# Turning and splitting the second layer's keys and queries in the latent stage instead of in the head loop

## The chip, the cores and the metric

The kernel runs on one core of a Trainium2 chip. The metric is the device time of one execution in microseconds; lower is better. The engines that matter are TensorE (PE; its weight loads are shown apart as PEld), VectorE (DVE), ScalarE (ACT), GpSimd (POOL) and SyncE (SP), which here does nothing but issue DMAs. ScalarE issues some DMAs as well, in line with its own work.

## What is computed

One step of a transformer trunk of two layers on 592 tokens: 512 prompt tokens, 64 sample tokens and 16 meta tokens. Layer 0 is a forgetting attention (16 heads of width 64) and an MLP. Layer 1 is a latent attention and an MLP. All of it is in f32, and every large product is made from operands split into a high and a low fp32r part, in three passes (high by high, high by low, low by high). Cut to what the change touches:

```python
def mla_shared_latent(x, kv_norm, w_kv_down, ckv_norm, pos):
    z = rmsnorm(x, kv_norm) @ w_kv_down
    ckv = rmsnorm(z[..., :KV_RANK], ckv_norm)            # KV_RANK = 256
    krope = rope(z[..., KV_RANK:], pos)                  # 32 columns, shared by all heads
    return ckv, krope
def mla_decompress(ckv, w_kv_up):
    kv = (ckv @ w_kv_up).reshape(bsz, t, MLA_HEADS, MLA_NOPE + MLA_V)   # 16, 64 + 64
    return kv[..., :MLA_NOPE], kv[..., MLA_NOPE:]
def mla_queries(h, w_q_down, q_norm, w_q_up, pos):
    cq = rmsnorm(h @ w_q_down, q_norm)                   # 384 columns
    q = (cq @ w_q_up).reshape(bsz, t, MLA_HEADS, MLA_NOPE + MLA_ROPE)   # 16, 64 + 32
    return q[..., :MLA_NOPE], rope(q[..., MLA_NOPE:], pos)
...
logits = (q_nope @ k_nope.T + q_rope @ k_rope.T) * MLA_SCALE
p = softmax(where(mask, logits, NEG));  o = p @ v;  x = x + o @ w_o_b
```

With the 256 cached rows there are 848 keys. The 592 query rows are worked in five units a head: four of 128 prompt rows and one of 80 (the sample and meta rows).

## The kernel before

Every engine runs a program of its own, in an order written out by hand, and the programs meet through semaphores. Large weights come in pieces j through four raw slots (`slot_of`); ScalarE makes the high part (`hi`), VectorE the low part (`lo`). Both layers run `attention(layer)` on each engine; only the step of a head differs.

**Layer 0.** The keys and queries of a head already lie turned (width on the partitions, tokens along the row) and split in DRAM (`k_turned`, `q_turned`). SP's `fox_head` loads kh, qh, kl and ql for head h into one of three slots, once TensorE is done with the head that had the slot. The step is `fox_step`: per head five score units, six groups of transposes of the probabilities, and the weighted sums of the heads before, all interleaved. Values of a pair of heads come straight from the cache and the outputs (`fox_v`, four DMAs, issued by ScalarE in the middle of a pair), and GpSimd splits them (`split_v`).

**Layer 1, latent stage.** After layer 0's MLP the stage makes the compressed latent and turns it (`ckvTh`, `ckvTl`). Then TensorE runs 28 products: for two weight pieces, seven token tiles by two blocks of 512 columns, tokens on the partitions, keys and values of a head side by side. ScalarE copies each out of PSUM to one of four slots of `stn`, and SP stores it to `kv_mla` in DRAM. After that fifteen transposes turn the query latent (`cqTh`, `cqTl`), and 20 products (four weight pieces by five token tiles, 384 columns, four heads each) give the queries; VectorE applies the rotary turn in `stn` with six small instructions, and SP stores to `q_mla`. At the end the rotary key `krn` is turned and copied into rows 64 to 95 of both kh slots.

**Layer 1, head loop.** SP loads natural rows for each pair of heads (`mla_q`, two DMAs; `mla_kv`, three, keys and values together). In `mla_step`, TensorE turns the next head's queries and keys with `prep`, twelve transposes in three groups, ScalarE copies each group (high part) and VectorE subtracts (low part). With the six groups of the probabilities these are the nine groups a head (`GROUPS = (6, 9)`). The steps run in hardware loops over the pairs. The output weights (`load_wo`) are loaded ahead of the loop.

## Time and profile before

| | |
|---|---|
| median of three runs | 1565.55 us (1563.05 to 1568.0) |
| profiled execution | 1566.23 us, span 1564.1 us, mean granted TensorE clock 0.972 |
| TensorE busy | 1480.1 us (95%), weight loads 1413.8 us (90%) |
| VectorE busy | 1081.4 us (69%) |
| ScalarE busy | 729.8 us (47%) |
| GpSimd busy | 432.4 us (28%) |
| DMA | 164.18 MB, mean 105 GB/s |

Times are positions on the profiled execution's clock or lengths in it, in us. The layers lie one after the other: attention of layer 0 about 185 to 360, its MLP after it, the latent stage of layer 1 from about 850, its attention about 947 to 1110, and the last MLP up to the end. The busy shares are means over all of these; the change touches the latent stage and the attention of layer 1 alone, so the views of those stretches are what counts. A row names the engine, the line of the kernel, the operation and its tiles (out <- in); PEclk is the granted clock as a share of full speed.

### The profile page before, as it was taken

Reading aid. Unit: us, or ns where it says so; the run is one execution under the profiler, and the core shown is the slowest. Engines: PE = TensorE matmul, PEld = TensorE weight load, DVE = VectorE, ACT = ScalarE, POOL = GpSimd, SP = SyncE. Lnnn points to the kernel's source line nnn. Section 1 sums busy time; section 2 is a strip of 40 time slices with the busy share of each in tenths; the row PEclk is TensorE's granted clock in tenths of the full one; section 3 lists DMA queues with packets and bytes.
Section 4 is the critical chain, followed back from the end, with each engine's and each line's share of the span. In section 5 each row is a group of like instructions: output and inputs, shape, how many; then the busy total and the mean of one; then the engine's idle time right before and its main releaser. Section 6 shows DMA issues by size and latency. Waiting matters only on the chain.

```text
span 1564.1 us, 29635 instructions
## 1 busy us (share of the span) xinstructions
PE 1480.1 (95%) x10389; PEld 1413.8 (90%) x10389; DVE 1081.4 (69%) x1962; ACT 729.8 (47%) x1510; POOL 432.4 (28%) x437
## 2 busy tenths in 40 slices
PE   8999988889899999999999997999989999999997
PEld 6788977779899999999988786999989999999997
DVE  5224267656987778787784156998598877878775
ACT  6234158754453433434252435998444343343434
POOL 0000047743422212222020004667342222222200
PEclk9999989989999999999999998999999999999998
DMA  8257566651131322313130637320022132231211
GB/s 289 99 145 210 147 186 167 165 138 48 55 109 55 106 92 68 107 54 107 56 132 19 227 121 201 94 77 1 29 81 99 64 107 82 78 107 64 97 54 61
DMA packets 129720, 164.18 MB, mean 105 GB/s; under 512 B 11936, under 2 KB 98912, under 8 KB 129648
## 3 DMA queue, kind: packets, MB, share of 16 engines
q1 hardware_dynamic: 124176, 160.62, 33.1%
q10 hardware_dynamic: 5472, 2.61, 0.9%
q8 instruction: 44, 0.72, 0.2%
q14 instruction: 28, 0.23, 0.0%
HBM read 132.52 MB, written 30.68 MB: 104 GB/s over the span
## 4 chain that ended last, share of the span: by engine, by line
PE 66%; issue 9%; DVE 7%; ACT 3%; DMA 3%; SPq 1%; POOL 1%; ACTq 0%; POOLq 0%; DVEq 0%
PE ps L2403 25%; PE ps L2434 21%; PE ps L1971 11%; PE ps L2137 3%; PE ps L2206 2%; PE ps L2250 1%; PE ps L2252 1%; SPq L574 1%; DMA ql<-q_turned 1%; DMA natv<-in_cache_v 1%; DVE wul L1701 1%; DVE wul L1410 1%; DVE bl L1747 1%; ACT pth L1085 1%; PE ps L2177 1%
## 5 line engine op out<-in xcount | busy, mean ns | idle before, releaser
L1799 DVE TENSOR_TENSOR xT<-xT,ps 128x592 f32<-128x592 f32 (+1 forms) x256 | 194.8, 761 | 49.0 <-PE ps L2403 47.2
L803 POOL TENSOR_TENSOR prob<-prob,rs 128x144 f32<-128x144 f32 (+4 forms) x160 | 119.4, 757 | 248.1 <-DVE rs L1562 246.5
L2434 PE MATMUL ps<-bh,wuh 128*128 128x296 f32 (+1 forms) x512 | 153.3, 299 | 8.6 <-DVE wul L1701 5.0
L2434 PE MATMUL ps<-bl,wuh 128*128 128x296 f32 (+1 forms) x512 | 152.9, 299 | 0.0
L2434 PE MATMUL ps<-bh,wul 128*128 128x296 f32 (+1 forms) x512 | 152.6, 298 | 0.0
L893 POOL TENSOR_TENSOR ssum<-raw 128x512 f32<-128x512 f32 x32 | 48.9, 1528 | 292.6 <-DMA raw<-in_w_up 290.1
L1572 DVE TENSOR_TENSOR ptl<-ps,pth 128x256 fp32r<-128x256 f32 (+2 forms) x192 | 96.1, 502 | 45.3 <-ACT pth L1085 44.6
L2403 PE MATMUL ps<-hh,dn2h 128*128 128x296 f32 (+1 forms) x512 | 111.6, 299 | 0.6 <-DVE xT L1799 0.3
L1267 ACT ACTIVATE snap<-ps 128x296 f32<-128x296 f32 (+1 forms) x32 | 13.2, 412 | 210.4 <-PE ps L2434 210.4
L2403 PE MATMUL ps<-hl,dn2h 128*128 128x296 f32 (+1 forms) x512 | 110.3, 296 | 0.0
L2403 PE MATMUL ps<-hh,dn2l 128*128 128x296 f32 (+1 forms) x512 | 110.2, 296 | 0.0
L2434 PEld LDWEIGHTS ps<-bh,wuh 128*128 128x128 f32 x512 | 96.7, 189 | 10.3 <-ACT snap L1267 4.5
L1085 ACT ACTIVATE pth<-ps 128x256 fp32r<-128x256 f32 (+2 forms) x192 | 84.4, 450 | 39.2 <-PE ps L2206 30.6
L1701 DVE TENSOR_TENSOR wul<-raw,wuh 128x512 fp32r<-128x512 f32 x128 | 97.4, 780 | 0.1
L2434 PEld LDWEIGHTS ps<-bh,wul 128*128 128x128 f32 x512 | 97.1, 190 | 0.0
L2434 PEld LDWEIGHTS ps<-bl,wuh 128*128 128x128 f32 x512 | 97.0, 189 | 0.0
L1255 ACT ACTIVATE hh<-hu 128x592 fp32r<-128x592 f32 (+1 forms) x64 | 44.4, 693 | 107.4 <-DVE hu L1786 107.4
L1971 PE MATMUL ps<-wh,xgh 128*128 128x512 f32 (+5 forms) x240 | 92.0, 383 | 2.5 <-DVE xT L1799 2.2
L1075 ACT ACTIVATE prob<-ps,nmx 128x144 f32<-128x144 f32 (+4 forms) x160 | 85.5, 535 | 18.5 <-DVE nmx L1556 15.2
L1971 PE MATMUL ps<-wl,xgh 128*128 128x512 f32 (+5 forms) x240 | 90.3, 376 | 0.0
L1971 PE MATMUL ps<-wh,xgl 128*128 128x512 f32 (+5 forms) x240 | 89.8, 374 | 0.0
L1556 DVE TENSOR_REDUCE nmx<-ps 128x1 f32<-128x144 f32 (+4 forms) x160 | 77.3, 497 | 15.4 <-PE ps L1971 14.4
(284 smaller groups left out, 4589.8 us busy)
## 6 DMA issues: line engine op xcount, KB each, us to landing
raw<-in_w_up SPq DMA_DIRECT2D x32, 1024.0 KB, 7.2
raw<-in_w_down SPq DMA_DIRECT2D x32, 1024.0 KB, 5.0
raw<-in_w_in_a SPq DMA_DIRECT2D x12, 1024.0 KB, 8.5
kh<-k_turned SPq DMA_DIRECT2D x32, 212.0 KB
k_turned<-kst SPq DMA_DIRECT2D x48, 128.0 KB, 2.5
kv_mla<-stn SPq DMA_DIRECT2D x24, 256.0 KB, 2.1
q_turned<-qst SPq DMA_DIRECT2D x32, 148.0 KB, 3.1
qh<-q_turned SPq DMA_DIRECT2D x16, 296.0 KB
```

Of the source, the lines that this page charges most:

```text
L803: g.tensor_tensor(prob[c][0:rows, off:off + n], prob[c][0:rows, off:off + n], rs[0:rows, u:u + 1].to_broadcast([rows, n]), ALU.mult).then_ ...
L893: g.tensor_tensor(ssum[:, 1 + 2 * par, :, :], a11, a21, ALU.subtract).then_inc(s_ready, 1)
L1075: s.activation(form(prob[c][0:rows, off:off + n]), src, ACT.Exp, bias=nmx[0:rows, u:u + 1], accum_out=sm[0:rows, u:u + 1]).then_inc(exp_do ...
L1085: s.activation(dst, src, ACT.Copy).then_inc(g_hi, 1)
L1556: v.tensor_reduce(nmx[0:rows, u:u + 1], logits(u)[0], AX.XY if u == NT - 1 else AX.X, ALU.max, negate=True).then_inc(max_done, 1)
L1572: v.tensor_tensor(dst, src, hi_part.bitcast(F32), ALU.subtract).then_inc(g_lo, 1)
L1701: v.tensor_tensor(up_unit(wul, u), up_source(u, par), up_unit(wuh, u).bitcast(F32), ALU.subtract).then_inc(ul_done, 1)
L1799: v.tensor_tensor(a, a, two_banks(2 + m % 2, n), ALU.add).then_inc(x_ready if last else acc_done, 1)
L1971: return te.matmul(out, a, b, start=start, stop=stop)
L2137: i = te.matmul(ps[:, 2 * q_banks(j) + t, 0:TH], w, x[:, k, TH * t:TH * t + TH], start=(k == 0 and p == 0), stop=(k == KD - 1 and p == 2), ...
L2403: i = te.matmul(ps[:, 2 * pair + t, 0:n // 2], w[:, k, c], x[:, k, t * (n // 2):(t + 1) * (n // 2)], start=(k == 0 and p == 0), stop=(k == ...
L2434: i = te.matmul(ps[:, bank, 0:h], w[:, k, :], x, start=(u not in (3, 4, 6) and k == 0 and p == 0), stop=(k == 3 and p == 2), skip_group_ch ...
```

## The change

The columns of `w_kv_up` and `w_q_up` are put in another order as the inputs are laid out, so that two heads' keys, two heads' plain queries, or four heads' rotary halves are 128 neighbouring columns. The key and query products then take the weights as the stationary operand and the latent as the moving one, so their results come out already turned: [128 = two heads of 64, 848 keys] and [128, 592 queries]. The values keep the old form.

**The stage** becomes one list, `LATENT`, of 34 items: eight key blocks (k) and fourteen value blocks (v) in turns, then four times two plain query blocks (n) and a rotary block (r). They use three pairs of PSUM banks, and an item waits for the item three before. For k and n ScalarE copies the high part and VectorE subtracts, into `lkst` (two slots) and `lqst` (three slots). For r VectorE does three multiplications by a table from DRAM (`rope`), an addition and, after ScalarE's copy, the subtraction. SP stores each k, n and r with four DMAs to `kTm`, `qTm` and `qRm`, each v with one to `v_mla`. The query latent is turned between the items 11, 13 and 15; the rotary key after 22, and its copies into three kh and kl slots come at item 23. SP's list has more in it: at item 27 it waits for the stores so far and loads heads 0 to 2, at item 30 the first two value pairs.

**The loop** drops `prep` and its groups, and both layers use one step in the order of `fox_step`, unrolled, with three slots of kh, kl, qh and ql. A head takes eight loads (`mla_head`), issued by SP when the head that had its slot has its scores. Value pairs from the third on are issued by ScalarE in the middle of a pair (`mla_v`, three DMAs). `load_wo(1)` comes after the last head's loads, its last three pieces after the last scores.

```diff
-GROUPS = (6, 9)
+GROUPS = (6, 6)
...
+        LATENT = []
+        for half in range(2):
+            LATENT += [(kind, i + (4 if kind == "k" else 7) * half) for kind, i in
+                       (("k", 0), ("v", 0), ("k", 1), ("v", 1), ("v", 2), ("k", 2), ("v", 3), ("v", 4), ("k", 3), ("v", 5), ("v", 6))]
+        for g in range(4):
+            LATENT += [("n", 2 * g), ("n", 2 * g + 1), ("r", g)]
+        LAST = {10: 0, 21: 1, 24: 2, 27: 3, 30: 4, 33: 5}
...
+        def lat_pair(n):
+
+            return (0, 1, 3)[n % 3]
...
             def load_wo(layer):
-                if layer == 1:
-                    sp.wait_ge(lo_done, W_END)
                 for m in range(KD):
-                    if layer == 0 and m == 5:
-                        sp.wait_ge(s_ps, 5 * (HEADS - 1))
+                    if m == 5:
+                        sp.wait_ge(s_ps, 5 * HEADS * layer + 5 * (HEADS - 1))
...
+            def mla_head(h, c):
+
+                sp.dma_start(kh[c][0:HD, :].bitcast(F32), kTm[0][h]).then_inc(kq_in[c], 16)
+                sp.dma_start(qh[c][0:HD, :].bitcast(F32), qTm[0][h]).then_inc(kq_in[c], 16)
+                for x in range(2):
+                    r = HD + 16 * x
+                    sp.dma_start(qh[c][r:r + 16, :].bitcast(F32), qRm[0][x, 16 * h:16 * h + 16, :]).then_inc(kq_in[c], 16)
+                sp.dma_start(kl[c][0:HD, :].bitcast(F32), kTm[1][h]).then_inc(kq_in[c], 16)
+                sp.dma_start(ql[c][0:HD, :].bitcast(F32), qTm[1][h]).then_inc(kq_in[c], 16)
+                for x in range(2):
+                    r = HD + 16 * x
+                    sp.dma_start(ql[c][r:r + 16, :].bitcast(F32), qRm[1][x, 16 * h:16 * h + 16, :]).then_inc(kq_in[c], 16)
...
+            for n, (kind, i) in enumerate(LATENT):
...
+                if kind == "v":
+                    t, c = i % 7, 512 * (i // 7)
+                    rows = TX if t == NT else P
+                    r0 = P * t if t <= NT else T + P * (t - 5)
+                    sp.wait_ge(v_evac, i + 1)
+                    sp.dma_start(v_mla[r0:r0 + rows, c:c + 512], stn[0:rows, i % 3, :]).then_inc(lv_out[i % 3], 16)
+                    continue
+                sp.wait_ge(kq_lo, kind_count("knr", n))
+                q = kind_count("nr", n) - 1
+                for low in range(2):
+                    if kind == "k":
+                        for p in range(2):
+                            sp.dma_start(kTm[low][2 * i + p], lkst[HD * p:HD * p + HD, i % 2, low, :].bitcast(F32)).then_inc(
+                                lk_out[i % 2], 16)
+                    elif kind == "n":
+                        for p in range(2):
+                            sp.dma_start(qTm[low][2 * i + p],
+                                         lqst[HD * p:HD * p + HD, q % 3, low, :].bitcast(F32)).then_inc(lq_out[q % 3], 16)
+                    else:
+                        for p in range(2):
+                            sp.dma_start(qRm[low][p, HD * i:HD * i + HD, :],
+                                         lqst[HD * p:HD * p + HD, q % 3, low, :].bitcast(F32)).then_inc(lq_out[q % 3], 16)
+                if n == 27:
+                    for i_ in range(2):
+                        sp.wait_ge(lk_out[i_], 64 * 4)
+                    for i_ in range(3):
+                        sp.wait_ge(lq_out[i_], LQ_COUNT[5][i_])
+                    sp.wait_ge(half_used, QU0 + 2)
+                    sp.wait_ge(kr_lo, 1)
+                    for h in range(3):
+                        mla_head(h, key_slot(h))
+                if n == 30:
+                    for i_ in range(3):
+                        sp.wait_ge(lv_out[i_], 16 * len(range(i_, 14, 3)))
+                    mla_v(sp, 0, 0, natv1[0])
+                    mla_v(sp, 1, 1, natv1[1])
...
-            mla_q(0, 0)
-            sp.wait_ge(kr_ps, 1)
-            mla_kv(1, 1)
-            mla_q(1, 1)
+            for i in range(3):
+                sp.wait_ge(lq_out[i], LQ_COUNT[11][i])
+            for h in range(3, HEADS):
+                sp.wait_ge(s_ps, 5 * HEADS + 5 * (h - 2))
+                mla_head(h, key_slot(h))
             load_wo(1)
...
+                for j in range(1, PAIRS - 1):
+                    step(2 * j, 0, j)
+                    act.wait_ge(v_split, PAIRS * layer + j)
+                    if layer == 0:
                         fox_v(act, j + 1, (j + 1) % 2, natv0[(j + 1) % 2])
-                        step(2 * j + 1, 1, j)
-                else:
-                    with act.Fori(1, PAIRS - 1) as i:
-                        step(2 * i, 0, i)
-                        step(2 * i + 1, 1, i)
+                    else:
+                        mla_v(act, j + 1, (j + 1) % 2, natv1[(j + 1) % 2])
...
+                    wait_lat(act, n)
...
+                    s.activation(lkst[:, i % 2, 0, 336:KEYS], ps[:, b, :], ACT.Copy)
+                    s.activation(lkst[:, i % 2, 0, 0:336], ps[:, b + 1, 0:336], ACT.Copy).then_inc(kq_hi, 1)
+                elif kind == "v":
...
+                if n == 23:
+                    act.wait_ge(kr_ps, 1)
+                    act.wait_ge(half_used, QU0)
+                    act.wait_ge(lo_done, QU0 + 2)
+                    for sl in range(3):
+                        s.activation(kh[sl][HD:R_MLA, 336:KEYS], pf[0:ROPE, 2048:2560], ACT.Copy)
+                        i_ = s.activation(kh[sl][HD:R_MLA, 0:336], pf[0:ROPE, 2560:2896], ACT.Copy)
+                    i_.then_inc(kr_T, 1)
...
+                elif kind == "r":
+                    wait_lat(dve, n)
+                    dve.wait_ge(rope_tab, 16)
+                    if i:
+                        dve.wait_ge(kq_lo, kind_count("knr", n) - 3)
+                    two = two_banks(lat_pair(n), T)
+                    for rows, src, tab, dst in ((slice(0, P), slice(0, P), 0, ra), (slice(0, HD), slice(HD, P), 1, rb),
+                                                (slice(HD, P), slice(0, HD), 1, rb)):
+                        v.scalar_tensor_tensor(halves(dst[rows, :]), two[src], MLA_SCALE, halves(rope[rows, tab, :]),
+                                               ALU.mult, ALU.mult).then_inc(qr_mul, 1)
+                    dve.wait_ge(qr_mul, 3 * i + 3)
+                    v.tensor_tensor(ra[:], ra[:], rb[:], ALU.add).then_inc(qr_ready, 1)
+                    dve.wait_ge(kq_hi, kind_count("knr", n))
+                    v.tensor_tensor(lqst[:, q % 3, 1, :], ra[:], lqst[:, q % 3, 0, :].bitcast(F32), ALU.subtract).then_inc(kq_lo, 1)
...
+            def latent_free(m):
+
+                kind, i = LATENT[m]
+                if kind == "v":
+                    pe.wait_ge(v_evac, i + 1)
+                elif kind == "r":
+                    pe.wait_ge(qr_mul, 3 * i + 3)
+                else:
+                    pe.wait_ge(kq_lo, kind_count("knr", m))
+
+            pe.wait_ge(zT_lo, 2)
...
-
-            pe.wait_ge(kr_ready, 1)
-            for t in range(NT):
-                te.transpose(pf[0:ROPE, 3072 + P * t:3072 + P * t + P], krn[:, t, :], ident)
-            for t in range(2):
-                te.transpose(pf[0:ROPE, 3584 + P * t:3584 + P * t + P], krn[:, 5 + t, :], ident)
-            te.transpose(pf[0:ROPE, 3840:3920], krn[0:TX, NT, :], ident[0:TX, 0:TX]).then_inc(kr_ps, 1)
+                if n == 22:
...
+                        return lambda k: view(w, j)[:, k, 512:1024]
+                    o = tokens_product(ps[0:r, bank, :], ((lambda k: ckvTh[:, k, c0:c0 + r]), (lambda k: ckvTl[:, k, c0:c0 + r])),
+                                       (values(wh), values(wl)), 2, r, 512)
+                else:
+                    def weights(w, k):
+                        a = view(w, j)[:, k, :]
+                        b = i % 4 if kind == "k" else 2 if kind == "r" else i % 2
+                        return a[:, P * b:P * b + P]
+                    x_h, x_l = (ckvTh, ckvTl) if kind == "k" else (cqTh, cqTl)
+                    spans = (slice(0, SEQ), slice(SEQ, KEYS)) if kind == "k" else (slice(0, TH), slice(TH, T))
+                    k_n = 2 if kind == "k" else 3
+                    for k in range(k_n):
+                        for p, (w, x) in enumerate(((wh, x_h), (wh, x_l), (wl, x_h))):
+                            for b, c in enumerate(spans):
+                                o = te.matmul(ps[:, bank + b, 0:c.stop - c.start], weights(w, k), x[:, k, c],
+                                              start=(k == 0 and p == 0), stop=(k == k_n - 1 and p == 2), skip_group_check=True)
+                o.then_inc(half_used if n in LAST else lat_ps, 1)
+                if n in (11, 13, 15):
+                    latent_query((n - 11) // 2)
+                if n == 22:
+                    turn_rope_keys()
...
+    kv = [h * 2 * HD + v * HD + d for g in range(2) for v in range(2) for h in range(8 * g, 8 * g + 8) for d in range(HD)]
+    q = []
+    for g in range(4):
+        heads = range(4 * g, 4 * g + 4)
+        q += [h * R_MLA + d for h in heads for d in range(HD)]
+        q += [h * R_MLA + HD + x * (ROPE // 2) + d for x in range(2) for h in heads for d in range(ROPE // 2)]
```

Each `...` above leaves lines out. `latent_query`, `turn_rope_keys` and `latent_free` are TensorE's; the first two hold the fifteen and the seven transposes of the code before.

## Rows read from the trace of the kernel before

**Rows 1.** Chain of waits that ended last: start us, length us, engine, tile, line.

```profile
196.14 6.58 PE ps L2137 x48
...
859.79 40.56 PE ps L1971 x168
```

**Rows 2.** Timeline of ScalarE: start us, length us, instruction, [idle before <- releaser].

```profile
333.76 1.06 ACT L970 ACTIVATE wuh<-raw 128x1024 fp32r<-128x1024 f32 x1 [1.55 <-DMA raw<-in_w_o_a]
...
952.76 0.38 ACT L1075 ACTIVATE prob<-ps,nmx 128x144 f32<-128x144 f32 x1 [2.28 <-DVE nmx L1556]
```

**Rows 3.** Timeline of TensorE; L1971 with a [idle] note is a head's first score.

```profile
325.72 0.34 PE L1971 MATMUL ps<-kh,qh 128*128 128x144 f32 x1 [1.33 <-DMA ql<-q_turned]
...
960.30 0.30 PE L1971 MATMUL ps<-kh,qh 96*128 96x144 f32 x1 [1.09 <-ACT prob L1075]
...
970.01 0.60 PE L2221 MATMUL ps<-cst,natq 128*96 128x128 f32 x4
...
970.76 0.36 PE L2250 MATMUL ps<-pth,vlh 128*128 128x256 f32 x1
...
1080.36 0.31 PE L1971 MATMUL ps<-kh,qh 96*128 96x144 f32 x1
```

**Rows 4.** Busy time by stretch: layer 0's heads 3 to 14, layer 1's 2 to 14, two steps of layer 0.

```profile
core 0: us, PE busy (x) PEld busy (x) DVE busy (x) ACT busy (x) POOL busy (x), PEclk, DMA share, GB/s
225.58:325.72 100.14, 86.73 (x675) 76.17 (x673) 74.24 (x208) 76.85 (x218) 70.56 (x98) 0.98 0.67 165
967.94:1080.36 112.42, 112.08 (x965) 107.98 (x964) 103.14 (x274) 103.86 (x287) 76.56 (x106) 1.00 0.21 64
233.80:240.98 7.18, 6.70 (x59) 6.25 (x58) 6.03 (x18) 6.35 (x19) 4.86 (x6) 1.00 0.60 155
240.98:250.16 9.18, 7.42 (x59) 6.17 (x57) 6.13 (x18) 6.36 (x18) 7.36 (x12) 1.00 0.70 173
```

**Rows 5.** Waits between 200 and 336 us: total us, times, longest us.

```profile
POOL vlh L826 <- DMA natv<-in_cache_v: 12.3, 6, 3.6
```

**Rows 6.** DMA issues of the page: KB each, median us from issue to landing.

```profile
natk<-kv_mla SPq DMA_DIRECT2D x8, 512.0 KB, 4.0
...
natv<-in_cache_v ACTq DMA_DIRECT2D x6, 128.0 KB, 13.6
...
q_turned<-qst SPq DMA_DIRECT2D x32, 148.0 KB, 3.1
qh<-q_turned SPq DMA_DIRECT2D x16, 296.0 KB
```

**Rows 7.** Groups by line and form: busy us, mean ns of one | idle before.

```profile
L1668 DVE TENSOR_TENSOR kl<-ps,kh 32x512 fp32r<-32x512 f32 x2 | 1.4, 677 | 0.2 <-ACT kh L1353 0.2
...
L1670 DVE TENSOR_TENSOR kl<-ps,kh 32x336 fp32r<-32x336 f32 x2 | 1.0, 488 | 0.0
...
L1352 ACT ACTIVATE kh<-ps 32x512 fp32r<-32x512 f32 x2 | 1.2, 578 | 0.2 <-PE ps L2553 0.2
...
L1391 DVE TENSOR_TENSOR wl<-raw,wh 128x1152 fp32r<-128x1152 f32 x4 | 5.2, 1350 | 0.0
...
L1786 DVE SCALAR_TENSOR_TENSOR hu<-hu,rT 128x592 f32<-128x592 f32 x32 | 26.7, 835 | 1.1
```

**Rows 8.** Timeline of SyncE's queue: start us, length of the issues us, tiles, count.

```profile
185.34 2.39 SPq L633 DMA_DIRECT2D q_turned<-qst  x4
187.90 0.48 SPq L521 DMA_DIRECT2D natv_first<-out_o_v_p  x1
...
196.57 0.42 SPq L524 DMA_DIRECT2D natv_first<-in_cache_v  x1
...
249.40 0.45 SPq L621 DMA_DIRECT2D kh<-k_turned  x1
249.89 0.60 SPq L622 DMA_DIRECT2D kh<-k_turned  x1
...
976.86 0.37 SPq L668 DMA_DIRECT2D natq<-q_mla  x1
```

**Rows 9.** Chain of waits: last partial sum of either attention.

```profile
354.05 1.44 POOL ol L845
...
1103.12 1.44 POOL ol L845
```

More of the change, by code:

```diff
@@ L719, in _ @@
             sp.dma_start(gq[:], io["q_norm"].partition_broadcast(P)).then_inc(rope_in, 16)
-            for j in range(QU0, W_END):
+            for j in range(QU0, QU0 + 2):
                 load(j)
@@ L1100, in out, with step @@
                     s.activation(corr[rows, :], pf[0:HD, 3072:3072 + T], ACT.Copy).then_inc(o_corr, 1)
-                def fox_step(h, c, pair, first=False, last=False):
+                def step(h, c, pair, first=False, last=False):
                     if first:
-                        act.wait_ge(half_used, KVD0 - 1)
+                        act.wait_ge(half_used, W_END if layer else KVD0 - 1)
                         for u in range(3):
                             exp(h, c, u)
-                        query_hi(PAIRS - 1)
+                        if layer == 0:
+                            query_hi(PAIRS - 1)
                         exp(h, c, 3)
@@ L1126, in fox_step @@
                     exp(h, c, 4)
-                def mla_step(h, c, pair, first=False, last=False):
-                    if not first:
-                        turned(h, 0)
-                    exp(h, c, 0)
-                    if not first:
-                        turned(h, 1)
-                    if not last:
-                        qk(h, 0, 1 - c)
-                        qk(h, 1, 1 - c)
-                    else:
-                        wo_high(layer, 0)
-                    exp(h, c, 1)
-                    if not first:
-                        turned(h, 2)
-                    if not (isinstance(h, int) and h < 2):
-                        out(h - 2, c, pair - 1)
-                    if not last:
-                        qk(h, 2, 1 - c)
-                    exp(h, c, 2)
-                    if not first:
-                        turned(h, 3)
-                    exp(h, c, 3)
-                    if not first:
-                        turned(h, 4)
-                        turned(h, 5)
-                    exp(h, c, 4)
-                step = mla_step if layer else fox_step
-                for k in range(3 * layer):
-                    qk(-1, k, 0)
                 step(0, 0, 0, first=True)
@@ L1355, in _ @@
+            for i in range(3):
+                act.wait_ge(lq_out[i], LQ_COUNT[11][i])
             attention(1)
@@ L1586, in out, with step @@
                                     ALU.subtract).then_inc(o_lo, 1)
-                def fox_step(h, c, pair, first=False, last=False):
+                def step(h, c, pair, first=False, last=False):
                     if first:
@@ L1592, in fox_step @@
                         clear_prob()
[L1593 removed]
+                        if layer == 0:
+                            query_lo(PAIRS - 1)
                         recip(h, 0)
@@ L1662, in clear_prob @@
                         v.memset(prob[c][:, P_OFF[NT] + 336:P_OFF[NT] + 384], 0.0).then_inc(p_zero, 1)
-                if layer == 1:
-                    clear_prob()
-                    dve.wait_ge(kr_T, 1)
-                    for sl in range(2):
-                        v.tensor_tensor(kl[sl][HD:R_MLA, 336:KEYS], pf[0:ROPE, 3072:3584],
-                                        kh[sl][HD:R_MLA, 336:KEYS].bitcast(F32), ALU.subtract)
-                        i = v.tensor_tensor(kl[sl][HD:R_MLA, 0:336], pf[0:ROPE, 3584:3920],
-                                            kh[sl][HD:R_MLA, 0:336].bitcast(F32), ALU.subtract)
-                    i.then_inc(kr_lo, 1)
-                step = mla_step if layer else fox_step
-                for k in range(3 * layer):
-                    qk(-1, k, 0)
                 step(0, 0, 0, first=True)
@@ L2263, in rest, with step @@
                 def rest(h, part, pair, vs, p):
-                    groups = p_split(layer, h - 1, 4 if part < 3 else 5) + G0
+                    groups = p_split(h - 1, 4 if part < 3 else 5) + G0
                     weighted_v(h - 2, part, groups, pair, vs, p)
-                def fox_step(h, c, pair, nat, turn=0, first=False, last=False):
+                def step(h, c, pair, nat, first=False, last=False):
                     if first:
-                        pe.wait_ge(kq_in[key_slot(0)], 80)
+                        pe.wait_ge(kq_in[key_slot(0)], kq_count(0))
                         for u in range(3):
                             scores(h, c, u)
-                        query_block(PAIRS - 1)
+                        if layer == 0:
+                            query_block(PAIRS - 1)
                         scores(h, c, 3)
```

522 lines of the change are left out of this document (201 added, 321 removed).

## The prediction

> **What bounds the kernel now.** I read the chain of waits first. It is TensorE almost everywhere, so the question is what happens to TensorE between the start of the latent products at 859.79 [rows 1] and the end of the second layer's attention. In between lie three parts. The products and their transposes run until about 940. Then comes a turn-over, in which the last queries go to DRAM, come back and are turned; the first exponential of the layer starts at 952.76 [rows 2]. Then the head loop: from head 1's first score at 960.30 to head 15's at 1080.36 [rows 3], 120.1 us for 14 heads, 8.58 us each. The stretch view says what sets that: in 112.42 us TensorE is busy for 112.08, VectorE and ScalarE for 103 [rows 4]. The loop is TensorE's own work. Next I read the same view over the first layer's loop, because the change gives the second layer that layer's order: 100.14 us for 12 heads, 8.35 each, with TensorE busy for only 86.73 [rows 4]. So that order, although it has less work for TensorE, is no faster; what it waits for has to be known before it is copied.
>
> **The loop after.** Removed per head: twelve transposes. Eight of them hold TensorE from 970.01 to 970.76 [rows 3], so twelve cost 1.1 us. The third pass of the scores stays. Weight loading is a count of TensorE's issue: 107.98/13 = 8.3 us a head; less 1.1 it is 7.2, and with the 0.2 to 0.3 that the loop has beyond it, the floor is 7.4 us. The first layer's good step shows the order itself: 7.18 us with 6.25 of weight loading [rows 4]. The second layer has 7.2 of it, about 0.95 more; the step had 0.48 us in which TensorE was idle for ScalarE and VectorE, and a later score covers most of it. I take 7.5 for a step without a value load.
>
> The other step of a pair takes 9.18 in the first layer [rows 4]. There ScalarE's queue issues four value loads, and GpSimd then waits for the last: 12.3 us in six times [rows 5], since it lands 13.6 us after its issue. The value loads of the second layer today land in 4.0 [rows 6]. The new ones lie between these ends. What holds the first layer's back is on the queue beside them: each head brings two loads of 68 partition rows, the new heads only loads of 64 and 16 rows. I take a landing near 4 to 6 us, so GpSimd has its values in time, a pair (some 15 us) being the lead. What is left is ScalarE's own issue of three loads, some 1.5 us by an estimate from SP's single issues of 0.4 to 0.5 [rows 8], of which the step can hide most: 7.9. The mean is 7.7, bounds 7.4 (TensorE's floor) and 8.3 (the first layer's pace). Fourteen heads: 107.8 against 120.1, a gain of 12.3; by the bounds 16.5 and 3.9.
>
> A rule of the Trainium skill bears on the 68 rows (page "DMA: Bandwidth & Descriptors", section on why a DMA increments its semaphore by 16): a copy is split over the largest number of engines up to 16 that divides its row count, which is 4 for 68 and 16 for 64 and 16. The 13.6 us agree with it; by the rule alone the loads land early and the loop goes to 7.7 or less, which is the value I have.
>
> **The latent stage.** Today 168 products of 512 columns take 40.56 us [rows 1], 0.241 each. After, 84 remain for the values (20.3 us), and the keys take 48 of 512 and 48 of 336 columns (19.2): 39.5. The fifteen query transposes move between products: 1.4 us at the rate above and some 1.3 of waiting for their splits. The first query product starts at 859.8 + 42.2 = 902.0. A query block is 18 products of 296 columns, 6.58/48 = 0.137 each [rows 1]: 2.5 us. Twelve of them are 29.6, no longer than today's query products.
>
> But now each block is also split, and VectorE does it in order. After the second block (907.7 with the seven key turnings, 908.4 with ScalarE's copy) it waits for the rotary keys: six copies on ScalarE, 3 x (0.58 + about 0.4) = 3.0, then 3 x (0.68 + 0.49) = 3.5 of its own [rows 7]: 914.9. A rotary block costs it three products, an add and a subtract of 592 columns, nearest row 0.835, with ScalarE's copy (0.7) and hand-overs between: 5.3. So the first rotary block ends at 920.2, two plain blocks at 0.835 give 921.9, a weight split 1.35 [rows 7] gives 923.2, the second rotary block 928.5. That is when the sixth block may be stored, item 27 of the list.
>
> **The queue behind it.** This decides, I think. SP takes its list in order, and at item 27 it has: 4 stores; a wait until they have landed; 24 loads for three heads; 12 stores of items 28 to 30; 6 value loads; 12 stores of items 31 to 33. ScalarE starts no exponential until the last store has landed, so all 58 lie on the path. The price of one: four stores of 64 rows in a burst took 2.39, and a load of 64 rows right behind another 0.60, with 0.04 between [rows 8]: 0.62. Lower end: single issues at 0.37 [rows 8], 0.41 with the gap. I take the burst, as this is one. Value loads: eight took from 187.90 to 196.99 in the first layer [rows 8], 1.14 each; alone 0.45; I take 0.8. A store lands 3.1 after its issue [rows 6]. From 928.5: stores 931.0, landed 934.1, 24 loads 949.0, 12 stores 956.4, values 961.2, 12 stores 968.6, landed 971.7. So the first exponential is at 971.7, not 952.76: 18.9 us later. At 0.41 each and 3.1 twice it is 928.5 + 30.0 = 958.5, 5.7 later. Without any queue, VectorE's own list would end near 943 and the last store land near 948, 5 earlier; that is the lower bound. TensorE meanwhile has the first three scores ready and stands. Behind SP wait the stores of items 31 to 33, but they find their staging slots free by then.
>
> **Head 0, tail.** From the first exponential to head 1's first score it takes 7.5 today [rows 2, 3], with the turnings of head 1 between; without them I estimate 4.5: the exponentials of 2 us, one double score at the low clock, one maximum and one more exponential. Gain 3.0 (0 to 3.5). At the end, the output weights, loaded ahead of the loop today, come behind head 15's loads. From head 15's first score to the last partial sum it is 22.8 today and 28.3 in the first layer [rows 3, 9], where ScalarE waited 1.55 for them [rows 2] with the last maxima and scores behind it. I take 2.0 of loss between 0 and 5.5, as the load of qh is 296 KB in the first layer [rows 6] and 96 rows of 592, 222 KB, after.
>
> **Sum.** 18.9 - 12.3 - 3.0 + 2.0 = +5.6 us. The profiled execution took 1566.23 us with a span of 1564.1; the median of three is 1565.55, so 0.7 lower. On the median: 1571 us.
>
> **Rivals.**
> - The queue is cheap (faster): an issue costs 0.41, not 0.62. For it: the value loads in today's loop are issued at 0.37 [rows 8]. Against it: those have another wait between them. 5.7 - 12.3 - 3.0 + 2.0 = -7.6: 1558. It decides for faster below about 0.43 a DMA, where 58 x 0.19 takes 11 us off and the sum passes -4.7.
> - The Trainium skill (page "DMA: Bandwidth & Descriptors", section on issuing engines not being separate queues) has it that issue time is "usually small relative to the DMA itself". The burst rows do not agree, since 58 of them are 36 us; by the rule the answer is this first rival.
> - The loop keeps the first layer's pace, 8.3: ScalarE's issue of the value loads delays every second step whatever the landing. For it: its queue holds four issues there and the step still shows 9.18. Against: nothing else stalls in the 7.18 steps. +18.9 - 3.9 - 3.0 + 2.0: 1580.
> - TensorE's floor in the loop, 7.4, and a tail without loss: 18.9 - 16.5 - 3.0 = -0.6: 1565, no change.
> - That the turning stays in some other form can't be: the twelve transposes have no successor in the loop.
>
> **Numbers.** About 0.3% (4.7 us) is what a measurement of this kernel can tell from no change. Forecast 0.50, and of its spread (1566 to 1577) about three fifths are beyond 1570.2; cheap queue 0.16; the pace of the first layer 0.16; the floor 0.18. Slower: 0.30 + 0.16 + 0.01 = 0.47. Same: 0.20 + 0.03 + 0.15 = 0.38. Faster: 0.13 + 0.02 = 0.15. The range goes from the cheap queue to a little above the first layer's pace, 1558 to 1582.
>
> **What would show it.** SP's timeline: a solid run of some 58 issues from about 928 to 969, at 0.6 each; at 0.4 the first rival holds. ScalarE's first exponential of the second layer near 972, and TensorE idle for some 10 us ahead of it. First scores of heads 1 and 15 some 108 us apart; steps that alternate 7.5 and 7.9, GpSimd without a wait for values. If it waits, the landing was misjudged; if the steps are equal and TensorE is full, the floor holds. ScalarE's wait for output weights below 1.5 us. The forecast is wrong if the stores and loads of SP go by unnoticed, or if the key and value products stall on their staging slots, which I hold for covered: 40 us hold some 50 issues.

## The result, and the profile after

Over 20 runs each, the changed kernel takes 1567.92 us (median) and the kernel before 1563.49: a ratio of 1.0029, interval 1.0019 to 1.0040, so 3.0 to 6.3 us more. The forecast was slower, 1571, +5.6 us.

The profiled execution spans 1564.7 us, only 0.6 more than that of before. Part of that is chance between two executions: the first latent product starts at 857.03, 2.76 earlier than in [rows 1], after work that is the same in both (in the thirteen traces of this case it starts anywhere from 853.2 to 859.8). From that product on the stretches can be set beside each other. First the chain of waits (start us, us, what):

```profile
857.03 4.13 PE ps L2486 x12
...
899.46 2.47 PE ps L2486 x18
...
916.37 0.45 SPq L771
916.86 0.60 SPq L771
...
926.08 2.46 DMA q_rope<-lqst
928.75 0.46 SPq L671
929.26 0.59 SPq L672
...
959.85 2.47 DMA q_rope<-lqst
962.47 0.95 ACT prob L1091 x4
...
1103.88 1.44 POOL ol L872
```

TensorE carries the chain through the query products that start at 899.46, up to 905.2. From there to 916.4 it runs through ScalarE and VectorE, which copy the rotary keys and make the first rotary block. From 916.37 on it is SP's queue without a break but for one landing, up to 959.85; then the last landing. The exponentials begin behind that. TensorE's timeline (as in [rows 3]) and two rows of ScalarE's (as in [rows 2]):

```profile
952.96 0.46 PE L1952 MATMUL ps<-kh,qh 96*128 96x144 f32 x1 [20.18 <-DVE rb L1917]
967.08 0.46 PE L1952 MATMUL ps<-kh,qh 96*128 96x144 f32 x1 [0.59 <-ACT prob L1091]
976.75 0.23 PE L1952 MATMUL ps<-kh,qh 96*128 96x144 f32 x1
...
1079.43 0.23 PE L1952 MATMUL ps<-kh,qh 96*128 96x144 f32 x1
```

```profile
962.47 0.38 ACT L1091 ACTIVATE prob<-ps,nmx 128x144 f32<-128x144 f32 x1 [8.12 <-DMA q_rope<-lqst]
...
1084.75 1.06 ACT L986 ACTIVATE wuh<-raw 128x1024 fp32r<-128x1024 f32 x1
```

The four rows are the first scores of heads 0, 1, 2 and 15. TensorE stood 20.18 us ahead of the first, and ScalarE 8.12 us for the last store to land. The high part of the output weights, at 1084.75, waited for nothing. The stretches, before and after (their sum and the 4.4 us between the medians differ by less than two executions of the same work do):

| from | to | before | after | moved | forecast |
|---|---|---|---|---|---|
| first latent product | first exponential | 92.97 | 105.44 | +12.47 | +18.9 |
| first exponential | head 1's first score | 7.54 | 4.61 | -2.93 | -3.0 |
| head 1's first score | head 15's | 120.06 | 112.35 | -7.71 | -12.3 |
| head 15's first score | last partial sum | 22.76 | 24.45 | +1.69 | +2.0 |
| sum | | | | +3.52 | +5.6 |

The loop, by stretches (as in [rows 4]): head 0's first scores, the step of head 1, a value step, a step without values, and heads 2 to 14.

```profile
core 0: us, PE busy (x) PEld busy (x) DVE busy (x) ACT busy (x) POOL busy (x), PEclk, DMA share, GB/s
952.96:956.30 3.34, 3.30 (x12) 2.76 (x12) 1.95 (x5) 0.70 (x1) 0.00 (x0) 0.50 0.90 277
967.08:976.75 9.67, 8.63 (x47) 8.33 (x48) 5.49 (x17) 5.82 (x18) 6.36 (x11) 0.68 0.41 104
1000.25:1008.10 7.85, 7.63 (x65) 7.03 (x63) 6.22 (x18) 6.37 (x18) 5.98 (x9) 1.00 0.74 171
1008.10:1015.83 7.73, 7.38 (x64) 7.07 (x63) 6.12 (x18) 6.34 (x18) 6.24 (x10) 1.00 0.44 115
976.75:1079.43 102.68, 97.72 (x808) 91.63 (x807) 79.25 (x218) 82.12 (x232) 77.74 (x111) 1.00 0.65 155
```

The first step ran at a granted clock of 0.68. The others alternate between about 7.73 and 7.85, but for one of 8.03 (from head 3) and two of 8.43 and 8.53. In one of these ScalarE's queue shows why (timeline):

```profile
1031.75 0.37 ACTq L527 DMA_DIRECT2D natv<-v_mla  x1
1032.15 0.52 ACTq L528 DMA_DIRECT2D natv<-v_mla  x1
...
1032.70 1.42 ACTq L529 DMA_DIRECT2D natv<-v_mla  x1
1034.17 0.38 ACT L1101 ACTIVATE pth<-ps 128x256 fp32r<-128x256 f32 x1 [1.80 <-PE ps L2187]
```

The three issues take 2.3 us, and ScalarE's next copy comes only after them. The view of DMA issues has their landing times (as in [rows 6]):

```profile
natv<-v_mla ACTq DMA_DIRECT2D x6, 256.0 KB, 3.8
...
natv<-v_mla ACTq DMA_DIRECT2D x6, 128.0 KB, 5.6
```

### The profile page after: what moved, and what is told of

Read it like the earlier page. It is cut to its first block, busy times and chain, and to the rows that moved or that the text cites. A ratio compares the mean times of both kernels' runs of the same rounds, so it can differ in the third digit from the quotient of the medians.

```text
span 1564.7 us, 28670 instructions
## 1 busy us (share of the span) xinstructions
PE 1459.8 (93%) x10245; PEld 1396.9 (89%) x10245; DVE 1063.7 (68%) x1824; ACT 702.5 (45%) x1442; POOL 431.5 (28%) x437
## 4 chain that ended last, share of the span: by engine, by line
PE 62%; issue 9%; DVE 7%; SPq 5%; DMA 4%; ACT 3%; POOL 0%; ACTq 0%; DVEq 0%; POOLq 0%
PE ps L2314 25%; PE ps L2345 21%; PE ps L1952 7%; DMA ql<-q_turned 3%; PE ps L2118 2%; PE ps L2187 2%; PE ps L2486 2%; PE ps L2213 2%; SPq L585 1%; PE ps L2215 1%; SPq L767 1%; DVE wul L1410 1%; DVE wul L1654 1%; ACT prob L1091 1%; DVE bl L1700 1%
## 5 line engine op out<-in xcount | busy, mean ns | idle before, releaser
L1952 PE MATMUL ps<-kh,qh 128*128 128x144 f32 (+5 forms) x192 | 67.5, 355 | 46.1 <-DVE rb L1917 20.2
```

What stands on the lines that cost most here:

```text
L1952: return te.matmul(out, a, b, start=start, stop=stop)
```

## The experiments

Each ratio is to the kernel before; the changed kernel's is 1.0029. "Below the changed kernel" is the difference of the ratios in us. "Stretch" is the time from the first latent product to the last partial sum in the profile: 243.33 before, 246.85 in the changed kernel. Its four parts, each from the end of the one before it, in us:

| run | to the first exponential | to head 1's first score | to head 15's | to the last partial sum |
|---|---|---|---|---|
| changed kernel | 105.44 | 4.61 | 112.35 | 24.45 |
| loads behind the stores | 94.18 | 5.28 | 114.17 | 23.12 |
| landing awaited elsewhere | 98.38 | 4.61 | 113.22 | 25.66 |
| one store a block | 98.50 | 4.61 | 113.05 | 24.33 |
| values issued by SP | 105.54 | 4.61 | 111.05 | 23.11 |
| two passes | 105.34 | 4.17 | 106.63 | 24.47 |
| products, first try | 106.95 | 4.61 | 111.09 | 24.47 |
| products, later gap too | 106.29 | 3.81 | 109.74 | 25.87 |
| all together | 85.73 | 7.78 | 111.09 | 24.45 |
| the same, four stores a block | 89.81 | 8.89 | 111.05 | 23.11 |
| head 1's loads earlier | 85.80 | 4.61 | 111.10 | 24.38 |
| the same, with products | 85.73 | 5.53 | 112.73 | 23.12 |

No edit but the two passes touches the tail, and yet it takes three lengths, which go with TensorE's granted clock in it: 23.1 us at 1.00 (four traces), 24.3 to 24.5 at 0.93 (six) and 25.7 to 25.9 at 0.87 (two). The changed kernel's, and that of the run with the values issued by SP:

```profile
1079.43:1103.88 24.45, 20.57 (x161) 19.87 (x159) 13.92 (x32) 13.96 (x32) 11.42 (x14) 0.93 0.38 109
1078.86:1101.97 23.11, 19.19 (x161) 18.32 (x159) 13.92 (x32) 13.96 (x32) 11.41 (x13) 1.00 0.40 113
```

So a difference in the last column is no effect of an edit that these runs could show, and each edit is judged by the part that it is about.

### The queue ahead of the first exponential

**Loads behind the stores.** The loads of heads 0 to 2 and of the first values move to the end of SP's list.

```diff
-                if n == 27:
+                if n == 33:
                     ...
                     for h in range(3):
                         mla_head(h, key_slot(h))
-                if n == 30:
                     ...
                     mla_v(sp, 0, 0, natv1[0])
```

> The 30 loads of heads 0 to 2 and of the first value pairs are issued behind the last store (item 33) instead of at items 27 and 30. Theory A (SP's list of issues, one after the other at about 0.63 us, is what holds up the first exponential): SP goes through the stores of items 28 to 33 right after item 27's, from 926.7 of the changed kernel's profile to about 942; head 0's eight loads take it to 947, landed 949; the first exponential comes near 951 instead of 962.5, and the time falls by 9 to 12 us against the changed kernel. Theory B (VectorE's list of splits is what ends late, as it does last before the scores at 954.4): the stores of items 28 to 33 are issued no earlier than now, the first exponential stays at 960 to 964 or comes later, since the loads now lie behind it, and the time does not fall.

Measured: ratio 0.9954 (0.9938 to 0.9970), 11.7 us below the changed kernel; stretch 236.75, 10.1 less. The first exponential is 94.2 after the first product, not 105.4. Theory A holds. The same 30 loads are issued one after the other as before, but only head 0's eight still stand ahead of the first exponential, which comes 11.3 us earlier. The loop takes 1.8 us more in this trace.

**The landing awaited elsewhere.** What the last stores still read is overwritten only by GpSimd's splits of the values, so GpSimd waits, not ScalarE.

```diff
-            for i in range(3):
-                act.wait_ge(lq_out[i], LQ_COUNT[11][i])
             attention(1)
...
                     head(j, j)
+                    if layer == 1 and j == 0:
+                        for i_ in range(3):
+                            pool.wait_ge(lq_out[i_], LQ_COUNT[11][i_])
```

> ScalarE's wait for the last store's landing ahead of the exponentials is moved to GpSimd, ahead of its first split of values, which is the write that would meet the stores' source. Theory A: the issue of the last twelve stores is on the path only through this wait, so that the first exponential comes at 956 to 957 (the maxima are ready at 955 to 957) instead of 962.5, and the time falls by 5 to 6 us against the changed kernel. Theory B (the end of VectorE's list sets it): the wait is no more than 1 to 2 us longer than the one that lies behind it, and the time falls by less than 2 us.

Measured: 0.9978 (0.9966 to 0.9990), 8.0 us below the changed kernel; stretch 241.87, 5.0 less. In this profile the wait ends at the maxima, as A has it, and the first exponential is 98.4 after the first product, 7.1 earlier, where 5.5 to 6.5 were expected. The stretch keeps 5.0 of it, since loop and tail happened to take 2.1 more; the interval of the runs is 2 us either way.

**One store a block.** High and low part and all 128 rows in one DMA; the tensors in DRAM are laid out so that its rows are neighbours.

```diff
-                for low in range(2):
-                    ...
-                        for p in range(2):
-                            sp.dma_start(qTm[low][2 * i + p],
-                                         lqst[HD * p:HD * p + HD, q % 3, low, :].bitcast(F32)).then_inc(lq_out[q % 3], 16)
+                    sp.dma_start((qT2 if kind == "n" else qR2)[:, rows, :].rearrange("l r n -> r l n"),
+                                 lqst[:, q % 3, :, :].bitcast(F32)).then_inc(lq_out[q % 3], 16)
```

> One thing alone: each block of keys or queries goes to DRAM in one store of 128 rows, high and low part together, where the change has four of 64 rows and one part. The bytes are the same, and the order of SP's list too. Theory A (SP pays for each DMA that it issues, 0.63 us): twelve stores on the path of the first exponential become three and three, so it comes some 12 us earlier, bounded by VectorE's splits to 6 to 10 us, and the time falls by 5 to 9 us against the changed kernel. Theory B (SP pays for the rows that it describes, some 0.01 us each: four stores of 64 rows cost what one of 256 does): one store takes about 2.5 us of SP, the first exponential stays within 1 us of 962.5 and so does the time.

Measured: 0.9980 (0.9967 to 0.9992), 7.7 us below the changed kernel; stretch 240.49, 6.4 less; the first exponential comes 6.9 earlier. SP's timeline:

```profile
916.59 0.36 SPq L764 DMA_DIRECT2D q_rope<-lqst  x1
...
924.10 0.36 SPq L764 DMA_DIRECT2D q_rope<-lqst  x1
...
940.60 0.94 SPq L764 DMA_DIRECT2D q_mla<-lqst  x2
```

against the changed kernel's

```profile
916.37 2.37 SPq L771 DMA_DIRECT2D q_rope<-lqst  x4
918.78 5.32 SPq L767 DMA_DIRECT2D q_mla<-lqst  x8
924.15 2.52 SPq L771 DMA_DIRECT2D q_rope<-lqst  x4
```

The bytes that took 2.4 to 2.7 us of the queue take 0.36 to 0.47 in one DMA (ten of the twelve query stores; the other two took 0.59 and 0.98). SP pays for each DMA, hardly for its rows: theory A. The landing grows in turn: a plain block of 592 KB lands in 5.1 us (median) where a store of 148 KB took 2.7. Two landings now lie on the chain of waits of this run, with ScalarE's copy and VectorE's last rotary block between them:

```profile
941.07 4.30 DMA q_mla<-lqst
...
951.64 3.97 DMA q_rope<-lqst
```

That is part of why 12 us of issue became 6.9.

### The loop

**Values issued by SP.**

```diff
-                    else:
-                        mla_v(act, j + 1, (j + 1) % 2, natv1[(j + 1) % 2])
...
                 mla_head(h, key_slot(h))
+                if h % 2 == 0:
+                    j = h // 2 - 1
+                    sp.wait_ge(v_split, PAIRS + j)
+                    mla_v(sp, j + 1, (j + 1) % 2, natv1[(j + 1) % 2])
```

> In the second layer's loop the three value loads of a pair are issued by SP, after the loads of a head, and no longer by ScalarE in the middle of a pair. Theory A (the loop's excess over 7.73 us a head is ScalarE's issue time): the steps of 8.43 and 8.53 us and those of 7.84 to 8.03 come down to about 7.73 each, fourteen heads lose some 2 us, and the time falls by 1.5 to 2.5 us. Theory B (those steps are long because the loads contend for the DMA engines, whoever issues them): the steps stay at 7.85 on average with one or two above 8.3, and the time stays within 0.5 us.

Measured: 1.0009 (1.0000 to 1.0018), 3.1 us below the changed kernel; heads 1 to 14 take 111.05 instead of 112.35, the stretch 2.5 less. The steps above 8.1 are gone but for the first, and the steps from head 5 on alternate. Those with values stay at 7.84 to 7.85 and those without at 7.72 to 7.74, so ScalarE's ordinary issue is not what makes the difference of 0.12.

The long steps are another matter: they are ScalarE's third issue where that takes long. In the six traces with three passes in which ScalarE issues the values, it took 1.24 to 1.68 us in eleven of 36 steps with values, and these are the eleven steps of 8.23 to 8.70. Where it took 0.45 the step is at most 8.04. On SP such an issue costs nothing: the second row here, of this run, lies in a step of 7.74 with one of 7.85 behind it. The first row is of the run below with products ahead of item 31, where ScalarE still issues the values:

```profile
1032.16 0.45 ACTq L529 DMA_DIRECT2D natv<-v_mla  x1
...
1044.51 1.34 SPq L529 DMA_DIRECT2D natv<-v_mla  x1
```

In that run none of ScalarE's issues was long, and heads 1 to 14 took 111.09 without any move. So the loop's 1.3 us here may be chance, and the stretch's other 1.3 are the tail at its full clock: the traces don't account for the 3.1 us between the runs. Half of theory A is shown, the mechanism of the long steps; what the move is worth is not. Why an issue is long now and then stays open.

**Two passes of the scores.** The pass of the low part of the queries by the high part of the keys is left out.

```diff
-                        passes = [(a_h, kh[i][0:R]), (a_h, kl[i][0:R]), (a_l, kh[i][0:R])]
+                        passes = [(a_h, kh[i][0:R]), (a_h, kl[i][0:R])]
```

> The third pass of the second layer's scores (low part of the queries by high part of the keys) is left out, so the scores are less precise; all else stays. Theory A (TensorE's own issue sets a step: 7.14 us of weight loading in 7.73): the step falls by the share of that pass, five score units with some 17 weight loads a head, about 0.95 us, to 6.8, and fourteen heads lose 12 to 14 us. Theory B (the chain from scores over maximum, exponential, normalising, turning and split sets a step, as it seems to do in the first layer): the step stays above 7.4 and the fourteen heads lose less than 5 us.

Measured: 0.9992 (0.9976 to 1.0008), 5.8 us below the changed kernel; heads 1 to 14 take 106.63, 5.7 less than in the changed kernel and 4.5 less than the 111.09 of a trace without long issues. Three stretches of it: a step with values, one without, and one where the clock fell.

```profile
999.91:1007.43 7.52, 7.24 (x58) 6.21 (x57) 6.12 (x18) 6.29 (x18) 5.96 (x9) 1.00 0.75 178
1007.43:1014.61 7.18, 6.70 (x58) 6.25 (x57) 6.03 (x18) 6.35 (x19) 6.24 (x10) 1.00 0.48 124
983.25:992.73 9.48, 8.44 (x59) 7.87 (x58) 6.04 (x18) 6.47 (x18) 4.54 (x8) 0.82 0.64 143
```

The step of 7.18 with TensorE busy for 6.70 and weight loads for 6.25 is that of the first layer to the last digit [rows 4]. So with two passes the order sets 7.18, and the third pass, 0.82 of weight loading and 0.68 of TensorE, makes it 7.73, 0.55 more. Neither theory holds alone: A has TensorE's share right and the size wrong, since with less work the chain between the engines takes over at 7.18. The chain of waits shows it: TensorE's own work is 80% of it around a step without values of the changed kernel (1007 to 1016), and 46% with two passes (1007 to 1015), where ScalarE's copies and VectorE's maxima come in.

### TensorE's clock after the wait

**Products into the gap, first try.** Useless products ahead of item 31 (60) and of the attention (12).

```diff
+                if n == 31:
+                    for _ in range(60):
+                        te.matmul(ps[:, 4, :], ckvTh[:, 0, 0:P], ckvTh[:, 0, 0:512], start=True, stop=True, ...)
```

> TensorE gets useless products whose result nobody reads, 60 ahead of item 31, where it stands for some 17 us in the changed kernel, and 12 ahead of the attention; all else stays. Theory A (the second layer's first two steps are long because TensorE comes out of the wait at half its clock, scores of 0.46 us where later ones take 0.23): the first scores take 0.23 to 0.3, the step from head 1 to head 2 falls from 9.67 to about 7.9, and the time by 2 to 3.5 us against the changed kernel. Theory B (the first steps are long because the pipeline of turnings and weighted sums has to fill): the step stays above 9.2 and the time within 1 us.

Measured: 1.0029 (1.0014 to 1.0045), no change, and the step from head 1 is 9.67 at a clock of 0.73. TensorE still stood idle between head 0's scores and the exponentials, and head 1's first score still took 0.46 us. This run did not put the question.

**Products into the later gap too,** 18 behind head 0's third unit and 5 behind the fifth.

> The changed kernel as it is, with useless products ahead of item 31 (60), ahead of the attention (12), behind head 0's third score unit (18, in the wait for the landing) and behind its fifth (5); the run with fillers only ahead of the scores had left that wait empty. Theory A (clock): head 1's first scores at about 0.23 to 0.3, the step from head 1 to head 2 near 7.8 instead of 9.67, 1.5 to 3 us less time than the changed kernel. Theory B (filling of the pipeline): the step stays above 9.2, the time within 1 us.

Measured: 1.0020 (1.0005 to 1.0035), 1.4 us below the changed kernel with intervals that overlap. The stretch view of the filled gap and of the step from head 1:

```profile
953.81:960.22 6.41, 5.82 (x19) 4.33 (x18) 1.28 (x11) 0.00 (x0) 0.00 (x0) 0.74 0.83 216
964.03:972.34 8.31, 6.20 (x48) 5.45 (x48) 5.40 (x17) 5.47 (x18) 6.36 (x11) 1.00 0.53 138
```

and TensorE's last wait in the step:

```profile
971.61 0.36 PE L2213 MATMUL ps<-pth,vlh 80*128 80x256 f32 x1 [1.57 <-DVE ptl L1572]
```

The step is 8.31 at full clock where it was 9.67 at 0.68. By this one trace the clock costs 1.4 us of the step's excess over some 7.8. The other 0.5 is probably the filling of the pipeline (TensorE waits 1.57 us for the last unit's split probabilities in it); no run separates it. The step's mean clock alone does not set its length: in nine traces it is 9.65 to 9.69 at means from 0.65 to 0.82. The loop is 1.35 shorter than in the first try (109.74 for 111.09, neither with a long issue), and the tail, at a clock of 0.87, gives 1.4 back.

### All together

**Merged stores, head 0 alone at item 27, the landing awaited by GpSimd, values from SP.**

> All together: merged stores; only head 0's loads at item 27, those of heads 1 and 2 and the first values behind the stores; the landing awaited by GpSimd; SP issues the loop's values. Theory A (the queue is the cost, and each of its places was found): the first exponential comes at 945 to 949 by the changed kernel's clock, the loop loses another 2 to 3, and the time is 15 to 20 us below the changed kernel, 11 to 15 below the kernel before. Theory B (VectorE's chain of rotary blocks and the hand-overs to ScalarE set the end once SP is out of the way): the first exponential stays near 951 as with the reordered loads, and the gain is 11 to 13 us against the changed kernel.

Measured: 0.9894 (0.9873 to 0.9915), 21 us below the changed kernel; stretch 229.05. The first exponential is 85.7 after the first product, at 942.8 by the changed kernel's clock. Theory A, with more gained ahead of the loop than it said (945 to 949) and less in it (1.3). The same with four stores a block:

> As the kernel with all together, but with the four stores a block that the change has. If SP pays per DMA, this one lies 3 to 6 us above it (first exponential some 4 us later, since head 0's loads and 24 stores are on VectorE's path through the staging slots); if it pays per row, the two are equal within 1.5 us.

Measured: 0.9938 (0.9920 to 0.9957), 6.9 us above the merged one, stretch 232.86, 3.8 above. Up to head 1's first score it is 5.2 behind, and the tail gave 1.3 back by its clock: per DMA again.

**Head 1's loads behind item 30.** TensorE stood 3.76 us for head 1's loads in the kernel with merged stores.

```diff
                     mla_head(0, key_slot(0))
+                if n == 30:
+                    mla_head(1, key_slot(1))
```

> The kernel with all together, where head 1's loads go out behind the stores of item 30 instead of behind the last store. In the kernel with all together TensorE stood 3.76 us for them ahead of head 1's first score. Theory A (SP's list is still the path there): that wait goes, head 1's first score comes 3 to 4 us earlier, and the time falls by 2.5 to 4 us. Theory B (the maxima and exponentials of head 0 or the values come next at once): less than 1.5 us of it is kept.

Measured: 1545.22 us, ratio 0.9880 (0.9864 to 0.9896), 17 us below the kernel before in the same series (1562.63), the lowest of all; stretch 225.89, 3.2 less than without this edit. By the stretch that is theory A; the runs with and without the edit (0.9880, 0.9894) have intervals that overlap. TensorE's timeline, heads 0 to 2:

```profile
940.00 0.46 PE L1949 MATMUL ps<-kh,qh 96*128 96x144 f32 x1 [8.24 <-DVE rb L1914]
...
947.12 0.46 PE L1949 MATMUL ps<-kh,qh 96*128 96x144 f32 x1 [0.59 <-ACT prob L1092]
...
956.07 0.36 PE L2210 MATMUL ps<-pth,vlh 80*128 80x256 f32 x1 [1.57 <-DVE ptl L1569]
```

The wait for loads is gone. What is left ahead of head 0 is a wait of 8.24 us that ends with a product of VectorE's last rotary block.

**With products in its gaps.**

> As the run before it, with useless products on TensorE where it stands: 26 ahead of the attention, 4 behind head 0's third score unit and 4 behind the fifth. Theory A (the granted clock of 0.5 that TensorE comes out of the wait with is what makes the first steps long): head 1's first scores take about 0.23 us instead of 0.46, the step from head 1 to head 2 falls from 9.69 to about 7.8, and the time by 2 to 4 us against the run without them. Theory B (the first step is long since its turnings and splits have to fill the pipeline): the step stays above 9.2 and the time is the same within 1 us or up to 2 us longer.

Measured: 0.9885 (0.9868 to 0.9902), no gain; the two are level. The clock was up for most of head 1's step and down one step later:

```profile
945.90:955.05 9.15, 7.05 (x47) 6.30 (x46) 5.34 (x16) 5.11 (x16) 6.12 (x11) 0.87 0.89 215
955.05:965.24 10.19, 9.82 (x63) 9.50 (x63) 5.36 (x14) 5.86 (x16) 6.35 (x11) 0.74 0.49 131
```

The step behind took 10.19 instead of 7.74. Neither theory is settled by this run; why the clock fell there stays open.

## Why the prediction was right

**The queue decides: right, too large by 6.4 us.** The step by which 58 DMAs at 0.62 lie on the path held in kind, and nearly in price: 12 stores in 7.63 us are 0.64 each, 24 loads in 13.34 are 0.56, six value loads in 3.14 are 0.52. What was too large: SP reached item 27's stores 67.1 us after the first product, not 68.7 (VectorE's rotary blocks took 4.7 to 4.8 us, not 5.3); the two landings ended 2.0 and 2.1 us behind the end of the last issue, not 3.1 (a landing of 3.1 in [rows 6] is counted from the start of the issue, as the 2.5 here is); the loads were 1.6 and the value loads 1.7 cheaper, and the stores 0.4 dearer. The cheap queue (0.41 each, 1558) is refuted. The Trainium skill's rule for that rival ("DMA: Bandwidth & Descriptors", section "Issuing engines are not separate DMA queues") is that issue time is usually small beside the transfer. It does not carry over to this burst: one issue, 0.59 us on average, is a quarter of the 2.5 us from a store's issue to its landing, but the landings overlap and the issues don't, so the 58 took 34.2 us of SP.

**One sentence of that part was wrong without effect on the time.** The staging slots of items 31 to 33 were not free: waits between 929 and 950 us show

```profile
ACT lqst L1334 <- DMA q_mla<-lqst: 16.9, 2, 15.0
```

ScalarE waits for SP's stores, which stand behind the loads. SP came to item 31's stores at 952.91 and found them ready, so it cost no time. But TensorE, forecast to stand for some 10 us, stood 20.2 ahead of head 0's scores because of it, and 7.2 more behind the first three of them. With SP's list shortened this loop of engines becomes the path, as the two landings in the run with merged stores show.

**The latent stage:** first query product forecast 42.2 after the first product, measured 42.43. **Head 0:** -2.93 for -3.0.

**The loop: right in kind, 4.6 us too good.** 112.35 for 107.8, the mis-sized term. The forecast took 7.5 for a step without values; it is 7.73. It took the third pass for almost hidden, and the run with two passes shows it at 0.55. That is 1.6 us over seven steps. The first step costs 1.9 more and was left out altogether, both its low clock and its filling. ScalarE's issue was put at "mostly hidden": true for 7.85, not for the two steps of 8.43 and 8.53 with a long issue, 1.2 us (other traces have none to three of these). The first layer's pace and the floor of 7.4 are both refuted, and GpSimd never waited for values; they landed in 3.8 to 5.6 us, as forecast.

**The tail: right in size by luck, wrong in cause.** +1.69 for +2.0, but ScalarE did not wait for the output weights. TensorE's busy time in the tail is 20.57 instead of 19.28 at a clock of 0.93 instead of 1.00. In the four traces in which the clock stayed at 1.00 the same tail takes 23.1 us, 0.35 more than before. So 1.3 of the 1.69 goes with the clock and about 0.35 with the new order; the wait that the 2.0 was made of did not occur.

So the forecast of the time (1571 for 1567.92, or +5.6 for +4.4) leans on two errors of 6.4 and 4.6 us with opposite signs: the direction and its cause, the queue, were right for the reason given; that the sum came this close was luck.

## What to carry to other kernels

A queue that issues is an engine with a program order: before moving work into DRAM and back, count the DMAs between the last result and its first use, here some 0.6 us each, and see what stands ahead of them. Merge stores across rows and parts first (0.4 us instead of 2.5 here), put loads in the order of their use, and let the engine that would overwrite the source wait for the landing, not the one on the path. Work that leaves a loop has to be priced at its new place: here 7.7 us gained in the loop met 12.5 lost ahead of it. With the queue ahead of the loop shortened as above, the changed kernel lies 17 us below the kernel before.

## What the runs showed of the hardware that was not expected

- The time that SP takes for an issue hardly depends on its size: mostly 0.36 to 0.47 us for 592 KB in 256 rows, mostly 0.60 for 148 KB in 64 rows.
- Now and then an issue takes 1.2 to 1.7 us instead of 0.4 to 0.5, on ScalarE's queue and on SP's. On ScalarE it lengthens the step of a head by 0.4 to 0.9 us, on SP by nothing.
- After the wait of 20 us TensorE came back at a granted clock of 0.50 (the level of 1.2 GHz), and the step from head 1 has a mean of 0.68 between the two levels, although it was busy for 8.6 of 9.67 us. In the run with two passes the clock fell to 0.82 in a step in which TensorE was busy for 8.44 of 9.48 us; in the step before it, at full clock, it had been busy for 6.73 of 7.19. What made it fall there, in the tail and behind the products is open.
